# A streaming encoder layer on one core: the first RMSNorm's root applied to the mixer's projections when they are evicted, memory keys and fill products moved in the delta stage

## What is computed

```python
def _rmsnorm(x, g):
    y = xf * lax.rsqrt(jnp.mean(xf * xf, axis=-1, keepdims=True) + EPS)
    return (y * g).astype(x.dtype)
...
h = _rmsnorm(x, norm_mix)
proj = jnp.einsum('bld,de->ble', h, w_in)      # pooling | q,k,v | a,b | z
pool_out, new_pool = _pool_mixer(u_pool, ...)
dn_out, new_conv, new_S = _deltanet_mixer(qkv, a, b, z, ...)
x = x + jnp.einsum('ble,ed->bld', jnp.concatenate([pool_out, dn_out], axis=-1), w_out)
...
m = _rmsnorm(mem, norm_mem)                    # 256 memory tokens
k = jnp.einsum('bmd,de->bme', m, w_mk); v = jnp.einsum('bmd,de->bme', m, w_mv)
```

## Time and profile before

| | us |
|---|---|
| median of 3 runs | 5200.41 |
| lowest and highest | 5194.11, 5201.63 |
| profiled execution, its own time | 5197.38 |
| its span, first to last instruction | 5195.3 |
| PE busy | 5011.6 (96%) |
| mean granted TensorE clock | 0.986 |

### The profile page before, as it was taken

The page is one execution under the profiler, slowest core; times in us unless marked ns, Lnnn a source line. Parts: engine busy times, 40 slices in busy tenths (PEclk is TensorE's granted clock), DMA queues, the critical chain, the costliest instruction groups (busy, mean ns, idle before and its releaser), DMA issues. The chain is left out here.

```text
span 5195.3 us, 93051 instructions
## 1 busy us (share of the span) xinstructions
PE 5011.6 (96%) x39028; PEld 4933.2 (95%) x39028; DVE 2420.4 (47%) x3520; ACT 1310.8 (25%) x1451; POOL 1327.7 (26%) x586
## 2 busy tenths in 40 slices
PE   6999999889999999999999999999999999999997
PEld 6999888789978999999999999999999999999997
DVE  3344454543222336577576767600444444444443
ACT  4234444422222312222111111122222122221222
POOL 1000042231000002343333333334332332233232
PEclk9999999999999999999999999999999999999998
DMA  3232433232333234332344434344333333333332
GB/s 114 91 145 106 149 108 103 78 133 89 123 135 111 86 117 153 110 129 104 118 151 134 151 134 151 134 168 156 119 137 140 133 130 136 137 123 140 140 119 79
DMA packets 233941, 651.23 MB, mean 125 GB/s; under 512 B 13696, under 2 KB 126720, under 8 KB 177024
## 3 DMA queue, kind: packets, MB, share of 16 engines
q1 hardware_dynamic: 233856, 650.03, 35.2%
HBM read 539.42 MB, written 110.56 MB: 125 GB/s over the span
## 5 line engine op out<-in xcount | busy, mean ns | idle before, releaser
L235 PE MATMUL pu<-xhi,whi 128*128 128x272 f32 x7456 | 1550.5, 289 | 39.7 <-DVE xlo L373 11.5
L235 PE MATMUL pu<-xhi,wlo 128*128 128x272 f32 x7456 | 1547.2, 289 | 0.0
L235 PE MATMUL pu<-xlo,whi 128*128 128x272 f32 x7456 | 1542.0, 288 | 0.0
L235 PEld LDWEIGHTS pu<-xhi,whi 128*128 128x128 f32 x7456 | 1176.0, 189 | 46.0 <-issue 30.4
L235 PEld LDWEIGHTS pu<-xlo,whi 128*128 128x128 f32 x7456 | 1176.4, 189 | 0.0
L235 PEld LDWEIGHTS pu<-xhi,wlo 128*128 128x128 f32 x7456 | 1168.9, 190 | 0.0
L219 ACT CAST whi<-raw 128x2048 fp32r<-128x2048 f32 x393 | 748.6, 1905 | 1514.9 <-PE pm L235 1184.3
L224 POOL TENSOR_TENSOR wlo<-raw,whi 128x2048 fp32r<-128x2048 f32 x128 | 607.2, 4743 | 1217.9 <-ACT whi L219 1217.9
L224 DVE TENSOR_TENSOR wlo<-raw,whi 128x2048 fp32r<-128x2048 f32 x265 | 611.3, 2307 | 458.5 <-ACT whi L219 450.2
L1438 POOL TENSOR_TENSOR clo<-coef,chi 128x544 fp32r<-128x544 f32 x124 | 261.7, 2130 | 995.1 <-ACT chi L1442 995.1
L1499 DVE TENSOR_TENSOR x<-pm,x 128x544 f32<-128x544 f32 x256 | 185.6, 725 | 584.0 <-PE pm L235 584.0
(11 more groups left out here) (288 smaller groups left out, 4953.7 us busy)
## 6 DMA issues: line engine op xcount, KB each, us to landing
raw<-units SPq DMA_DIRECT2D x393, 1024.0 KB, 4.8
h_s<-h_out SPq DMA_DIRECT2D x128, 272.0 KB, 2.1
gate_s<-table SPq DMA_DIRECT2D x17, 2048.0 KB, 9.5
h_in<-h_s SPq DMA_DIRECT2D x32, 1088.0 KB, 7.2
gate_in<-gate_s SPq DMA_DIRECT2D x32, 1088.0 KB, 9.2
q_s<-q_out SPq DMA_DIRECT2D x32, 320.0 KB, 2.2
x<-xT SPq DMA_DIRECT2D x8, 1088.0 KB, 5.3
qh<-q_s SPq DMA_DIRECT2D x8, 1088.0 KB, 7.3
```

Of the source, the lines that this page charges most:

```text
L235: ins = nc.tensor.matmul(out, w, xs[b][m == 1], start=(first and n == 0 and m == 0), stop=(last and n == len(terms) - 1 and m == 2))
```

## The change

- **First norm.** The products of the mixer run on x times gain, split as before, without the root. The sum over partitions stands inside product 1 (before its k = 12). The root, `scale` (544 columns, kept as `scale_kept` from the q/k/v stage on), is multiplied into each result at eviction, which DVE does now in the z, a/b, pooling and q/k/v stages. For z, DVE writes `z_in` and ACT then takes Silu of it. The first block only issues loads, in another order (`vecs` first, `consts` last); squares and splits run in the second block, four tiles at a time. PE waits for `consts` before product 0.
- **Memory norm.** The sum stands inside unit 17 (before k = 8) instead of between units 15 and 16. The tiles are split in units 18 to 22, by 4, 3, 3, 3, 3; that part is unrolled.
- **Memory keys.** Four of the eight units (`BEHIND` = 4) run at the end of the q/k/v block; in the delta block four are left, and the decays of chunk 0 come after the last.
- **Chunks.** Fill 0 stands behind the scores, each later fill half a level earlier; none is left behind P of level 6. ACT's copy of the first half of `v_out` moves from level 4 to level 3. The load of `S_sample` is issued in chunk 3, ahead of the wait for that chunk's output; PE waits for it before ks of the sample chunk instead of before the scores.

```diff
+            pe.wait_ge(set_loaded, 16)
+            unit_product(pe, Z_AT, 0, before=lambda k: pe.wait_ge(next_lo, k + 1))
+            unit_product(pe, Z_AT + 1, 1, before=total)
...
+            split_hi(act, 0, 1, 0)
+            act.wait_ge(vecs_loaded, 16)
+            for j in range(4):
+                act.wait_ge(x_loaded[j], 16)
+                for k in range(4 * j, 4 * j + 4):
+                    nc.scalar.activation(xhi[:, k], x[:, k], ACT.Copy, scale=gain(k)).then_inc(next_hi, 1)
+                for k in range(4 * j, 4 * j + 4):
+                    act_square(act, x, k, k % 2, T, 0)
+            ahead(0, 0)
+            act.wait_ge(total_ready, 1)
...
+            nc.scalar.activation(scale, scale, ACT.Exp, scale=-0.5).then_inc(scale_ready, 1)
+            ahead(0, 1)
+            gated(0, 0)
+            gated(0, 1)
...
+            def scaled_z(i, s):
+                u, slot, _ = unit(Z_AT, i, s)
+                finished(dve, u + 1)
+                nc.vector.tensor_tensor(in_two(z_in[s]), both(slot), in_two(scale), ALU.mult).then_inc(psum_free, 1)
...
+            for j in range(4):
+                for k in range(4 * j, 4 * j + 4):
+                    dve.wait_ge(next_hi, k + 1)
+                    nc.vector.scalar_tensor_tensor(xlo[:, k], x[:, k], gain(k), xhi[:, k].bitcast(F32), ALU.mult, ALU.subtract).then_inc(next_lo, 1)
+                for k in range(4 * j, 4 * j + 4):
+                    sum_squares(dve, k, k % 2, T, 0, nc.vector)
+            ahead(0, 0)
+            dve.wait_ge(scale_ready, 1)
+            scaled_z(0, 0)
+            ahead(0, 1)
+            scaled_z(0, 1)
...
     def act_qkv(act, u, slot, i, s):
         j = 2 * i + s
-        finished(act, u + 1)
...
-        nc.scalar.copy(ext[:, s, 3:3 + HALF], pu[:, slot, 0, 0:HALF])
...
+        finished(dve, u + 1)
+        dve.wait_ge(hist_kept, 2 * i + PRIME)
+        nc.vector.tensor_tensor(ext[:, s, 3:3 + HALF], pu[:, slot, 0, 0:HALF], scale_kept[:, 0:HALF], ALU.mult)
+        nc.vector.tensor_tensor(ext[:, s, 3 + HALF:3 + TP], pu[:, slot, 1, 0:TP - HALF], scale_kept[:, HALF:TP], ALU.mult)
...
+    MEM_TILES = {18: range(0, 4), 19: range(4, 7), 20: range(7, 10), 21: range(10, 13), 22: range(13, 16), 23: ()}
...
+            def total(k):
+                if k == KT // 2:
+                    pe.wait_ge(mem_summed, KT + 2)
+                    nc.tensor.matmul(pm[:, 0, 0, 0:M], ones, mem_sum[:], start=True, stop=True).then_inc(total_ready, 1)
...
+            pe.wait_ge(mem_lo, KT)
+            for n in range(BEHIND):
+                u, slot = MK_AT + n, (MK_AT + n) % 2
+                pe.wait_ge(lo_ready, u + 1)
+                pe.wait_ge(psum_free, u + 1)
+                products([pu[:, slot, 0, 0:M]], [(whi[:, slot, k], wlo[:, slot, k], [(memhi[:, k], memlo[:, k])]) for k in range(KT)]).then_inc(tiles_done, 1)
...
@@ pe_chunk @@
             ins.then_inc(q["scores"], 1)
+        if ahead:
+            pe_fill(pe, c, 0)
         pe.wait_ge(sso_read, c + PRIME)
...
             ins.then_inc(q["turned"], 1)
+        if not ahead:
+            pe.wait_ge(q["s_loaded"], 16)
...
         for l in range(1, levels):
             if ahead:
-                pe_fill(pe, c, 2 * l - 2)
+                pe_fill(pe, c, 2 * l - 1)
...
             if ahead:
                 pe_ahead(pe, c + 1, l)
-                pe_fill(pe, c, 2 * l - 1)
+                if l < levels - 1:
+                    pe_fill(pe, c, 2 * l)
...
@@ SP, chunk(c, last) @@
+                if last:
+                    sp.wait_ge(v_stored, 16 * sample + PRIME)
+                    sp.dma_start(S_sample[:], a["state"].rearrange("h p n -> p h n")).then_inc(q["s_loaded"], 16)
                 sp.wait_ge(cat_done, 2 * c + (2 + PRIME))
```

More of the change, by code:

```diff
@@ L54 @@
 AHEAD = 8
+BEHIND = 4
 FILL_AT = MK_AT + AHEAD
@@ L470, in build @@
-    norm_mix = Norm(x, V_MIX, T, xhi, xlo)
     place = region(WR, W_SIZE)
@@ L758, in _ @@
                     unit_product(pe, u, slot)
-            pe.wait_ge(mem_summed, KT + 2)
-            nc.tensor.matmul(pm[:, 0, 0, 0:M], ones, mem_sum[:], start=True, stop=True).then_inc(mem_total, 1)
-            with pe.Fori(HALF_WAY, LAST + 1) as i:
+            for s in (0, 1):
+                u, slot, _ = unit(QKV_AT, HALF_WAY, s)
+                unit_product(pe, u, slot, before=total if s == 1 else None)
+            with pe.Fori(HALF_WAY + 1, LAST + 1) as i:
                 for s in (0, 1):
@@ L894, in residual_and_projection @@
         counts["squares"] += KT
-        rows = run * KT
+        rows = (run + 1) * KT
         base2 = base + KT
@@ L2017, in _ @@
             load_z(0, P)
-            for n in range(AHEAD):
+            for n in range(BEHIND, AHEAD):
                 u = MK_AT + n
@@ L2025, in _ @@
             chunk(sample - 1, True)
-            sp.wait_ge(v_stored, 16 * sample + PRIME)
-            sp.dma_start(S_sample[:], a["state"].rearrange("h p n -> p h n")).then_inc(q["s_loaded"], 16)
             finished(sp, OUT0 - Z0)
```

356 lines of the change are left out of this document (158 added, 198 removed).

## The result

| us | before | after |
|---|---|---|
| median | 5200.76 | 5162.07 |
| lowest and highest | 5194.11, 5201.63 | 5160.58, 5162.69 |
| profiled execution, its own time | 5197.38 | 5162.69 |
| its span | 5195.3 | 5160.9 |

The ratio is 0.9928 (95% interval 0.9911 to 0.9945): the change makes the kernel 0.7% faster, 38.7 us by the medians and 34.7 between the two profiled executions. The forecast was 5164.

What follows compares the result with a forecast made beforehand. PE was taken to bound the kernel, busy 5011.6 of 5195.3 us. Terms -9.8, -6.7, +1.8, -12.0 and -9.7 made -36.4 on 5197.4, so 5161.0; adding 3.0 for the median gave 5164, range 5148 to 5182.

Steps and rivals of the forecast that it cites:

- Head: First norm and z products: product 0 needs no root, product 2 starts at 61.8 against 74.5; -9.8 us after clock and eviction.
- Moved evictions: Scaled evictions moved from ACT to DVE: about 0.95 us where ACT took 0.83; +0.2, hidden in the units' slack.
- q/k/v: q/k/v stage: the 6.0 us wait on the memory's sum and 2.0 of low clock go, a new wait comes; -6.7.
- new wait at unit 19: q/k/v stage: the root delays the next split beyond the product covering it; 0.9 us, 1.1 with the low clock.
- Keys and chunk 0: Moved memory keys and chunk 0: new key waits, later preparation, fill 0 gain and fill 4 wait; +1.8 us.
- second transposes at t + 77.0: Chunk 0, t being the end of product 23: preparation behind the last key makes A come 3.3 us later than t + 73.7.
- wait ahead of fill 4: Each chunk: fill 4 is due before its lower split ends, a new wait of 1.5 us.
- Chunks 1 to 3: Each chunk gains 1.5 us of idle time and 2.5 of clock, 4.0 in each; -12 in all.
- the 1.3 left of the wait for A: Chunks 1 to 3: the 4.29 us wait shrinks by a fill of 3.0, and the clock is expected to stay up.
- Rival 1: Clock does not recover in the chunks: costs 7.5 us there, up to 5 in chunk 0 and keys; 5175, chance 0.20.
- window mark of 97: Sign in the trace: chunk windows of 97 us, not 94, would mean the clock had not recovered in the chunks.
- Sample chunk: Earlier state load and PE's wait behind the scores: the 12.7 us wait goes, -11.2, less 1.5 for low clock; -9.7.

Runs made afterwards that it cites:

- Run 1: Kernel after, with the sum over partitions and the wait for the root back ahead of product 0 in the head; 5167.85 us.
- Run 2: Kernel after, with unit 1 split ahead of the last four squares and sums, unit 2 ahead of the root, PE's sum at k = 8; 5148.41 us.
- run 6: Kernel after, with each q/k/v unit's two large evictions done a second time on DVE, in sequence; 5166.17 us.
- run 8: Kernel after, with PE's sum of the memory's squares back between units 15 and 16; 5170.08 us.
- Run 4: Kernel after, with the load of S_sample back behind chunk 3 and PE's wait for it left at its new place; 5167.77 us.
- run 5: Kernel after, with no memory keys moved (BEHIND = 0, all eight units in the delta block); 5161.75 us.
- run 9: Kernel after, with key unit 1's split ahead of the last convolution and Silu, and DVE's q, k, v wait behind its delta-block splits; 5162.53 us.
- run 7: Kernel after, with DVE's split for fills 4 and 5 ahead of the residual's operations at level 1; 5152.48 us.
- run 12: Kernel after, with the new head order and fill 4's split ahead of the residual, without the key orders; 5139.29 us.
- run 3: Kernel after, with the fills at their old places and ACT's copy of the first half of v_out back at level 4; 5169.91 us.
- run 10: Kernel after, with the new head order, fill 4's split ahead of the residual and the two key-wait orders together; 5143.56 us.
- run 11: Kernel after, with head, fill 4 and key-wait orders together, plus key unit 2's load issued ahead of the last q/k/v store; 5138.24 us.

## Why the prediction held, point by point

**Head (-9.8 forecast, -9.2 measured).** The mechanism held step by step: product 1 at 40.8 (42.3), product 2 at 59.9 (61.8), z's end at 134.8 (136.2), the block's gap 0.8 longer. Three sizes were off. The chain of ACT and DVE ran 1.5 us ahead of my placing, mainly a pass of four tiles in 6.5 and not 6.9. Lower clock that I did not have came behind z: 1.5 in PE's busy time for the a/b and pooling stage (136.70 to 138.23), where only the gap was forecast. And the waits ahead of products 1 and 2 were 5.6 and 4.0 where I had 7 each. The second is shorter because product 1 was slow: it took 15.1 (40.78 to 55.87) where I had about 12.5, and PE spent at the lower clock part of what it would have waited. Run 1 adds what the prediction didn't split: half of z's gain comes from the new order of the splits and from products that run in one go, not from the root. Run 2 shows that what was forecast to be given back (the two waits with their clock) was given back only by the order of the splits and the place of the sum.

**Moved evictions (within slack).** Right. The four pieces took 0.44, 0.40, 0.16 and 0.18, 0.92 from first to last, against 0.95 forecast, and run 6 shows what a whole extra eviction costs. The Trainium skill ("VectorE: DVE Perf Modes", the TRN2 errata) gives (120 + 272) cycles at 0.96 GHz for the first piece, an estimate of 0.41 us: the trace agrees within 0.03. 

**q/k/v (-6.7, measured -6.3).** The wait and its clock are 8.0, by the medians of run 8 as by the sum. By the profiles the idle part came (6.0 to 0.5 us) but only 0.7 of busy time went, since the trace of after holds 2.8 of lower clock ahead of unit 19 that runs 4, 5 and 9 don't have. That the two totals agree within 0.4 is luck in part. The new wait at unit 19 was 0.44, not 0.9: the convolution ended 0.5 earlier behind its product than I had it, and the root took 3.5, not 2.9.

**Keys and chunk 0 (+1.8, measured +0.2).** The part of the sum that put the second transposes at t + 77.0 is the one that failed: they came at t + 73.5, 0.2 sooner than before, with fill 0 in front of them. The waits were 3.2, 3.2 and 3.0 where I had 4, 3.8 and 5, and PE waited 0.5 for A. From that step alone the move of the keys was a cost of 3.3; by run 5 it is worth nothing in either direction that could be measured. The wait ahead of fill 4 was 1.31, forecast 1.5. What used up the gain behind the transposes was clock, which the sum put at nothing here: chunk 0 went from 1.00 to 0.98 and PE's busy time in it from 87.3 to 89.1. Taking the wait ahead of fill 4 away did not bring it back (run 7, 88.8), while in run 12, where the chunk is the same as in run 7, it is 87.2. It falls behind the waits of 1.7 and 0.6 ahead of the first products P, which run 12 has too; why only in one of them stays open.

**Chunks 1 to 3 (-12, measured -7.1).** This is the term that was mis-sized. Its idle part held: 23.5 of idle time became 20.0, -3.6 where -4.5 was forecast; the wait for A fell from 4.3 to 1.5. The clock part did not: -7.5 forecast, -3.5 measured (270.94 to 267.45 busy), because the clock was still 0.98 in every chunk. Not all of the 7.1 is the fills' place either: by run 3 it is worth 3.9, 2.4 idle and 1.4 clock. I had reasoned that the 1.3 left of the wait for A would be too short to bring it down. That reasoning is the step that failed: in chunks 1 and 2 the clock falls right behind the 1.5 that is left (0.83 over the ten us from 729.0), and in chunk 3 behind the waits of 1.7 and 0.6 ahead of the first products P. Yet the length of that wait does not settle it: run 7 takes away the 1.31 ahead of fill 4, leaves the 1.5 for A, and the three chunks run at 1.00, as do all but one of runs 10 to 12. So the wait that the change itself had added, which I priced at its own length, went with another 1.8 in each chunk, though the clock does not fall behind it. Rival 1 was half right: by its window mark of 97 it fell, by the clock it described what happened. The Trainium skill ("TensorE: Matmul & The Clock Gate", HAM oscillation) has waits between groups of matmuls bring the clock down again and again; the chunks of the kernel after agree with it (0.98), while those of run 7 show that not every such wait does: at 1.00 they still hold waits of 1.5, 0.7, 1.7 and 0.6.

**Sample chunk (-9.7, measured -11.7).** The 12.7 wait became 4.25 for A, as forecast, and the transposes came 8.0 behind the end of chunk 3 in place of 19.1: -11.1 where I had -11.2. I charged 1.5 for clock behind the new wait, and nothing of it came: from the transposes to the output projection it is 47.1, and was 47.6. The old wait had its own clock, too, which stood ahead of the transposes: the scores behind it took 6.4 (1043.70 to 1050.06), and take 3.7 now (1008.64 to 1012.38). Run 4 divides the gain into 7.0 for the load's place and 4.6 for PE's wait behind the scores, which the prediction didn't keep apart.

The sum came out right partly because its errors cancelled, and that is luck: 4.9 too much gain in the chunks and 2.0 too little loss behind z, against 1.4, 1.6 and 2.0 too little gain in z, at the keys and in the sample chunk. The last step cancelled once more: I added 3.0 because the median of before stood above its profiled execution, but after the change the profiled execution was the slowest of the four, 0.6 above the median. For that execution the sum gave 5161.0, and it took 5162.7.

## What to carry over

Price a wait of the busiest engine at its length plus what the clock does behind it, and do so for a small new wait as well as for the large one removed: taking 1.3 us ahead of a fill away gave 3.3 in three chunks of four here. Look in short windows for the place where the clock falls, since it need not be the wait that was edited. When a wait is taken away, ask what lands next, and what the new order pushes back: the wait ahead of key unit 1 covered a load that was issued behind a store, and the edit made that store later still. And when a dependency is taken off a path, move the work that stood behind it too; the splits left behind the squares and the root in the head, and the sum's late place, held back 13.7 us, more than a third of what the whole change brought. Last, compare busy time stretch by stretch before an effect of 2 or 3 us is laid to an edit: stretches that no edit touched differed by as much.

## What the runs showed of the hardware that I had not expected

The clock stays up in chunks that still hold short waits: 1.00 with 1.5, 0.7, 1.7 and 0.6 us (run 7, chunks 1 to 3). It falls in chunks with one more of 1.3 (0.98, the kernel after), but 12 to 25 us ahead of that wait, behind one of the others. No wait's length alone decides it: the wait of 1.5 for A had the clock fall behind it in chunk 1 of the kernel after, and not in chunk 1 of runs 2, 7 and 9. And the same 317 matmuls of the sample chunk took 40.6 to 41.5 us of busy time in the kernel after and ten of the runs, but 44.8 in run 11 and 46.2 in run 3, by the granted clock alone; I found no edit that explains it.
